# Four elementwise products of each head pair on GpSimd instead of VectorE, in a fused RWKV-7 and pooling layer on one core

## The reference, cut to what matters

```
z = h @ w_in                                  # columns r, k, v, g_rwkv, u_pool, g_pool, ...
r, k, v = token-shifted mixes of z
decay = exp(-0.606531 * sigmoid(w0 + tanh(xw @ w1) @ w2));  a = sigmoid(a0 + (xa @ a1) @ a2)
S_t = S_{t-1} diag(decay_t) + (S_{t-1} a_t) b_t^T + v_t k_t^T ;  o_t = S_t r_t
y_a = (group_norm(o) * ln_w + ln_b + bonus) * silu(g_rwkv)     # silu(g) = sigmoid(g) * g
```

## Time and profile before

| | us |
|---|---|
| median of 3 runs | 1145.81 |
| lowest and highest | 1145.09 and 1146.93 |
| the profiled execution, whole | 1146.05 |
| its span from first to last instruction | 1144.5 |

### The profile page before, as it was taken

How to read it: one execution, slowest core, us unless ns; L and a number is a source line. 1 busy time by engine, 2 the same in 40 slices (tenths; PEclk the granted TensorE clock), 3 DMA queues, 4 the chain that set the end, 5 groups by cost and what they waited for, 6 DMA issues and landing times.

```text
span 1144.5 us, 23678 instructions
## 1 busy us (share of the span) xinstructions
PE 1117.6 (98%) x8594; PEld 1072.2 (94%) x8594; DVE 794.6 (69%) x1681; ACT 543.7 (48%) x960; POOL 159.7 (14%) x273
## 2 busy tenths in 40 slices
PE   5999999999999999999999999999999999999998
PEld 5889998999999999999999999999999999989998
DVE  5979897979798888988678544444444497685442
ACT  5444747566574747474643333333333343354342
POOL 2422131314131221221140000000000500000000
PEclk9999999999999999999999999999999999999999
DMA  9714433434343343443464555555555965516551
GB/s 239 199 38 124 122 104 111 113 110 115 110 128 97 107 127 99 115 121 103 129 184 130 152 147 154 153 144 149 147 148 147 283 186 148 149 54 167 168 161 38
DMA packets 279708, 155.10 MB, mean 136 GB/s; under 512 B 7717, under 2 KB 275661, under 8 KB 279012
## 3 DMA queue, kind: packets, MB, share of 16 engines
q1 hardware_dynamic: 272528, 139.65, 43.6%
q0 software_dynamic: 6992, 14.87, 4.9%
q10 hardware_dynamic: 148, 0.04, 0.0%
HBM read 149.15 MB, written 5.61 MB: 135 GB/s over the span
## 4 chain that ended last, share of the span: by engine, by line
PE 70%; DVE 17%; issue 6%; DMA 4%; ACT 3%; DVEq 0%; SPq 0%; ACTq 0%; POOL 0%; POOLq 0%
PE acc L1753 14%; PE acc L1755 13%; PE acc L1754 13%; PE wide L1755 6%; PE wide L1754 6%; PE wide L1753 6%; PE wide L1777 4%; DVE wl L1116 3%; PE wide L1860 2%; PE wide L2157 2%; DVE rn L1221 1%; PE wide L1772 1%; DMA wraw<-in_w_out 1%; ACT wh L719 1%; DVE kkn L1511 1%
## 5 line engine op out<-in xcount | busy, mean ns | idle before, releaser
L1116 DVE TENSOR_TENSOR wl<-wraw,wh 128x1024 fp32r<-128x1024 f32 x256 | 315.8, 1240 | 168.6 <-ACT wh L719 166.5
L719 ACT CAST wh<-wraw 128x1024 fp32r<-128x1024 f32 x256 | 266.8, 1048 | 213.3 <-PE acc L1755 124.0
L1753 PE MATMUL acc<-hh,wh 128*128 128x320 f32 (+1 forms) x1084 | 349.4, 322 | 8.6 <-DVE rS L1132 5.6
L1754 PE MATMUL acc<-hl,wh 128*128 128x320 f32 (+1 forms) x1084 | 336.5, 310 | 0.0
L1755 PE MATMUL acc<-hh,wl 128*128 128x320 f32 (+1 forms) x1084 | 335.8, 310 | 0.0
L1753 PEld LDWEIGHTS acc<-hh,wh 128*128 128x128 f32 x1084 | 204.2, 188 | 13.1 <-issue 7.4
L1754 PEld LDWEIGHTS acc<-hl,wh 128*128 128x128 f32 x1084 | 204.1, 188 | 0.3
L1755 PEld LDWEIGHTS acc<-hh,wl 128*128 128x128 f32 x1084 | 204.1, 188 | 0.0
L1753 PE MATMUL acc<-x1h,wh 128*128 128x320 f32 x256 | 81.0, 316 | 0.0
L1753 PE MATMUL acc<-mh,wh 128*128 128x320 f32 x256 | 79.4, 310 | 0.2 <-DVE wl L1116 0.2
L1755 PE MATMUL acc<-x1h,wl 128*128 128x320 f32 x256 | 79.1, 309 | 0.0
(11 more groups left out here) (424 smaller groups left out, 2003.7 us busy)
## 6 DMA issues: line engine op xcount, KB each, us to landing
wraw<-in_w_in SPq DMA_DIRECT2D x160, 512.0 KB, 3.8
wraw<-in_w_branch SPq DMA_DIRECT2D x32, 512.0 KB, 4.0
wraw<-in_w_out SPq DMA_DIRECT2D x32, 512.0 KB, 4.3
wraw<-in_w_ple_gate SPq DMA_DIRECT2D x32, 512.0 KB, 4.2
xt<-in_x_prompt SPq DMA_DIRECT2D x2, 1024.0 KB, 7.2
S0n<-in_state_wkv POOLq DMA_DIRECT2D x64, 32.0 KB, 3.6
out<-so POOLq DMA_DIRECT2D x16, 128.0 KB, 4.1
xt<-in_x_prompt POOLq DMA_DIRECT2D x2, 1024.0 KB, 7.8
```

What stands on the lines that cost most here:

```text
L719: A.copy(wh[:, slot, :], wraw[:, slot, :]).then_inc(s["hi_ready"], 1)
L1116: V.tensor_tensor(wl[:, slot, :], wraw[:, slot, :], wh[:, slot, :].bitcast(F32), ALU.subtract).then_inc(s["lo_ready"], 1)
L1753: M.matmul(out[:, 0:width], wh[:, slot, wcol], hi, start=first, stop=False)
L1754: M.matmul(out[:, 0:width], wh[:, slot, wcol], lo, start=False, stop=False)
```

## The change

Four VectorE instructions of each step go to GpSimd, and the waits go with them:

- The low part of `go(4)` is made by GpSimd behind its parameter copy, and that of `go(10)` behind its two small low parts. Since `lo_ready` counts in order, GpSimd waits until VectorE has done the chunk before, and VectorE waits at `go(5)` and `go(11)` until GpSimd has done the one before those.
- The output product `yf` is made by GpSimd behind the issue of the stores, and it waits for its end (`y_done`) together with the stores.
- The gate product `sg` is made by GpSimd at the start of the next step, behind `cur_p` and its waits. The exponential `pd` on ScalarE now waits for it (`sgs_ready`), as `pd` overwrites `dO`, which `yf` reads, and so does the product `bU` on VectorE.

```diff
@@ GpSimd, mix(r)
                 wait_alone("acc_free", r * TILES_STEP + (ACC_STEP + TILES_STEP))
+                wait_alone("sg_ready", r + 1)
+                gp_.tensor_tensor(sg[:, :], sgt[:, :], gS[:, :], ALU.mult).then_inc(s["sgs_ready"], 1)
@@ GpSimd, mix_out(r)
+            def split_low(r, j):
+                at_chunk = (r + 1) * CH_STEP + BASE_STEP + j + AHEAD
+                slot = (j + AHEAD) % SLOTS
+                wait_alone("lo_ready", at_chunk)
+                wait_alone("hi_ready", at_chunk + 1)
+                gp_.tensor_tensor(wl[:, slot, :], wraw[:, slot, :], wh[:, slot, :].bitcast(F32), ALU.subtract
+                                  ).then_inc(s["lo_ready"], 1)
             def mix_out(r, q=None):
+                split_low(r, 4)
                 wait_alone("tails_ready", r * 8 + 4)
...
                     lora_low(q)
+                split_low(r, 10)
                 wait_alone("end_ready", r + 1)
...
+                wait_alone("dve_step", r * 3 + 3)
+                gp_.tensor_tensor(yf[:, ds(r * T, T)], dO[:, :], sg[:, :], ALU.mult).then_inc(s["y_done"], 1)
                 wait_alone("eout", r * 32 + 32)
                 wait_alone("sout", r * 32 + 32)
+                wait_alone("y_done", r + 1)
@@ ScalarE, mix
                 A.activation(pi[:, :], cl[:, :], ACT.Exp, scale=DECAY).then_inc(s["exp_ready"], 1)
+                act.wait_ge(s["sgs_ready"], r + 1)
                 A.activation(pd[:, :], cl[:, :], ACT.Exp, scale=-DECAY).then_inc(s["exp_ready"], 1)
@@ VectorE, mix
+                def go_after_gpsimd(j):
+                    dve.wait_ge(s["lo_ready"], q * CH_STEP + (BASE_STEP + j + AHEAD))
+                    go(j)
-                dve.wait_ge(s["sg_ready"], r + 1)
-                V.tensor_tensor(sg[:, :], sgt[:, :], gS[:, :], ALU.mult).then_inc(s["sgs_ready"], 1)
...
+                dve.wait_ge(s["sgs_ready"], r + 1)
                 V.tensor_tensor(bU[:, :], kkn[:, :], aS[:, :], ALU.mult).then_inc(s["bh_ready"], 1)
...
-                go(4)
-                go(5)
+                go_after_gpsimd(5)
...
-                go(10)
-                go(11)
+                go_after_gpsimd(11)
...
-                dve.wait_ge(s["dve_step"], r * 3 + 3)
-                dve.wait_ge(s["sgs_ready"], r + 1)
-                V.tensor_tensor(yf[:, ds(r * T, T)], dO[:, :], sg[:, :], ALU.mult).then_inc(s["y_done"], 1)
```

## The result

The changed kernel took 1194.58 us (median of 4 runs, 1191.97 to 1196.78) against 1145.45 for the kernel before in the same session (4 runs, 1144.85 to 1146.93). The ratio is 1.0426, with an interval of 1.0402 to 1.045: slower by 49.1 us. The forecast was 1162 and its range ended at 1180, so the sign was right and the time was not. The profiled execution, the fastest of the four, has a span of 1190.4 us, 45.9 us more than that of the kernel before.

What follows compares the result with a forecast made beforehand. TensorE, busy 98%, was taken as the bound, with other engines mattering only where it waits. 0.75 + 1.5 = 2.25 us at seven boundaries, 15.8 us, on 1145.8 gave 1161.6, forecast 1162; range 1155 to 1180.

Steps and rivals of the forecast that it cites:

- The bound: Whole kernel: TensorE is busy 98%; VectorE and GpSimd matter only where TensorE waits, about 6.4 us.
- the exclusion: VectorE products of two SBUF tensors and GpSimd instructions hold each other off; VectorE products with a PSUM operand aren't held.
- The order in the middle: Low part of go(4), mid-step: VectorE's small product L1399 goes ahead of GpSimd's split, so TensorE loses 0.
- the first rival: Mid-step: GpSimd goes ahead of L1399, out(1) comes 2.0 us late in eight steps, 16 more, 1177 us; chance 0.27.
- `go(10)`: End of step: dsq_l stands for GpSimd's low part, and TensorE waits 0.75 us a boundary.
- `yf`: Output product on GpSimd: takes 0.73 us, hidden by the wait for the stores; cur_p wants to start at 329.5.
- `sg`: Start of step: gate product delays pd by 3.2 us and sq_l by 2.6; TensorE waits 1.5 us a boundary.
- the second rival: Start of step: gate product runs behind go(0); TensorE's wait is 2.55 instead of 1.5 us, 1169 us; chance 0.12.
- The sum: Between steps: 0.75 + 1.5 = 2.25 us at each of seven boundaries, 15.8 us in all, forecast 1162.

Runs made afterwards that it cites:

- `go(4)` alone: Kernel before the change, with only the low part of go(4) moved to GpSimd: 1176.06 us, ratio 1.0274.
- all but `go(4)`: The whole change with the low part of go(4) given back to VectorE: 1168.49 us, ratio 1.0205 against the kernel before.
- the gates alone: Kernel before the change, with only the output product yf and gate product sg moved to GpSimd: 1161.13 us, ratio 1.0137.
- the run with quarters: Kernel before the change, with only the low part of go(4) on GpSimd, as four instructions of 256 columns: 1148.14 us, ratio 1.0027.

## Why the prediction was wrong, step by step

- **The bound, the exclusion.** Right. TensorE's waits set the larger part of the price, VectorE was not relieved, and every late row above is a product of two SBUF tensors that stood for one on GpSimd, or what was queued behind it.
- **The order in the middle: the step that failed.** "I take this order by a hair" put VectorE's small product first and the cost at 0. VectorE came as forecast, 0.41 us behind `go(3)`. GpSimd's two waits took 0.34 us, not the 0.43 read from the earlier trace rows, and this was enough. What came is the first rival, at its price plus the longer duration: 2.15 us a step, not 2.0. The margin in the rows was 0.02 us and the stake 16 us; a forecast that hangs on this is no better than its coin.
- **The clock: a term that was missing.** The sum took each wait at its own length. The granted clock stood in no term, though waits of 1.5 us, and of 2.6 to 2.8 in the rivals, were forecast, longer than any in the earlier trace rows. It added 7 to 9 us net (16 before what the later waits gave back), and about 13 with `go(4)` alone. Even the first rival's 1177 lacked the clock. Waits of 1.1 and of 0.8 us brought none.
- **`go(10)`.** The mechanism held to the row. 0.75 us was mis-sized by the duration alone: 128x1024 on GpSimd took 2.37 us, not 2.0, and 0.75 + 0.37 is the 1.12 to 1.14 measured. The figure of the Trainium skill (page GPSIMD Engine Reference, section 3.1), from which I had estimated 2.25, was nearer. It also comes in all eight steps, not seven; the last has a `dsq_l` too.
- **`yf`.** It took 0.87 us, not 0.73. That `cur_p` would wait for the landing of the stores was wrong: its row names `yf`, 0.71 us before it, and the end of `yf` plus the waits in a row explains it.
- **`sg`.** The order was that of the second rival: behind `go(0)`, which VectorE, relieved of two products, reached early. Measured from TensorE's `dsq_h`, `pd` began at 353.49 - 340.92 = 12.57 us instead of 328.72 - 319.27 = 9.45, with the 1.14 that is 4.3 us late and not 3.2. The sum's own way from there holds: less 0.65 and 0.2 us of slack and the 1.14 it makes 2.3 us, and 2.4 to 2.5 were lost at the products with `zr`, near the rival's 2.55. TensorE stood for 1.79 of it at `sq_l` already, where it had about 0.7 us to spare. That this wait alone is near the 1.5 is luck: the term was too small by 1 us a step.
- **The sum.** The boundaries made 9.1 + 11.0 = 20.1 us where the forecast had 15.8, though the last of the seven cost only 0.28 for `sq_l`: there, behind the loop, `sg` got in before `go(0)`. The 0.7 us by which the gates cost more than the `sq_l` wait add 4.2 in six steps. With 17.2 for the middle (8 x 2.15, no `rS` wait shortened) and 7.4 for the clock it is 48.9 of the 49.1 measured. The range ended at 1180 because its upper end had only the first rival with a longer duration; the case in which the middle, the gates and the clock all go wrong together was not in it.

## What to carry to other kernels

Where a wait of TensorE hangs on which of two engines asks first, treat both orders as possible and price the bad one in full, with the clock that such a wait can cost behind it. Work that goes from VectorE to GpSimd is not gone from VectorE: where VectorE's next products have both operands in SBUF, they stand for GpSimd's duration, which is the longer one. So put it behind the next deadline and beside work on PSUM, or cut it into short instructions. And before a wait is removed, look at what is next in the same queue: taking away 0.8 us a step brought nothing until `go(4)` moved too.

## What was not expected of the hardware

- GpSimd's product of two operands takes 2.37 us for 128x1024 and 0.87 us for 128x320 (group means 2372 and 870 ns). The 128x512 of `xp` and `zr` takes 1.05 us, less than half the first and little more than the second; the line through the earlier trace rows, which gave 1.9 (I took 2.0) and 0.73, doesn't hold for these products. Why wasn't tried.
- A wait of TensorE of 1.8 to 3.0 us was followed by 3.4 us at half clock in 10 of 14 cases of the changed kernel; with `go(4)` alone in all eight waits of 2.9 us, once for 6.8 us; but with all but `go(4)` in only 1 of 6 waits of 1.8 us, and with the gates alone in 2 of 6. What decides among equal waits stays open. A stretch behind a `sq_l` wait left the step as long as without it, one behind an `rS` wait made it 1.4 to 1.5 us longer.
- Between two GpSimd instructions that follow each other at once, a waiting VectorE product gets in, after 0.75 us in the run with quarters.
